# Gate and up projections of a SwiGLU FFN: 2x2 block products of seven half products, with weight sums on GpSimd

## The chip, the cores and the metric

One core of one Trainium2 chip runs the whole program. The metric is the device time of one launch in microseconds (us), lower is better. The kernel before was timed in three runs. TensorE is PE in the profile (PEld is its weight load), VectorE is DVE, ScalarE is ACT, GpSimd is POOL, SyncE is SP; an engine's name with a q is its queue of DMA issues.

## The reference, cut to what matters

A decoder layer works on 2048 prompt rows and on 32 sample rows (8 sequences of 4 tokens), with 1024 features. The part that changes is the FFN, hidden width 2816 (22 tiles of 128):

```python
gate, up = jnp.split(_rmsnorm(h, g_ffn) @ w_ffn_in, [D_FF], axis=-1)
y = h + (jax.nn.silu(gate) * up) @ w_ffn_out
```

Before it stand a norm, one input projection, sliding-window attention beside a gated linear recurrence (the mixers), and an output projection; after it a final norm.

## The kernel before

**Blocks.** Features lie on the 128 partitions and positions on the free axis. The prompt is worked in NB = 4 blocks of T = 512 positions. The 32 sample columns ride along as columns 512 to 543 in two places: in the first block's head (the `head(0, True)` of the five engines' programs: q, k and v of the samples are computed there and wait in columns T:W) and in the last block's mixers, output projection and FFN. A block of W = 544 columns is called wide, and each of its products is made in two halves of 272 columns.

**Units.** All dense products are units: 128 output features, `kt_of[u]` input tiles (8, or 7 or 8 in the down projection). A block has 90 of them: 6 in the head (k, v, four q), 8 in the mixers, 8 of the output projection (`U_O`), and the FFN in three chunks (`FCH` = 8, 7, 7 hidden tiles): for every hidden tile one gate unit and one up unit (`U_IN`), then eight down-projection units (`U_OUT`). Numbers are 32-bit: each operand is split into a high part (fp32r, made by ACT) and a low part (the rest, made by DVE), and an input tile takes three matmuls, high by high, high by low, low by high (L533 to L535 in `gemm`). A unit of eight tiles is thus 24 matmuls of 512 columns, or 48 of 272 in a wide block.

**Weights.** SP loads each unit's 512 KB into one of two buffers of `w_raw` (L404), ACT copies it to `w_hi` (L883, a ring of three), DVE subtracts it to `w_lo` (L1157). On ACT and DVE the split of unit u + 3 stands behind the work on unit u, in an order written out by hand. Semaphores count up and each engine waits for fixed counts.

**FFN.** PE runs the units without other work between (`ffn`, on PE). DVE takes the gate unit out of PSUM while it multiplies by `rinv`, the inverse root mean square (L1170), ACT takes the tanh (L1099), DVE makes tanh + 1 times gate (L1553), takes out up (L1170), multiplies (L1557), ACT and DVE split the result into `a_hi` (L1102) and `a_lo` (L1561). The down projection is added to `hT` (L1563).

**Output projection.** DVE adds bias and residual (`hT`, L1406); `h_tile` squares it on ACT (L907), adds the squares on DVE (L1180) and splits g * h into `x_hi` (L908) and `x_lo` (L1194), the FFN's input. `rinv` comes later, from a product of the summed squares with ones (`feature_sums`, L544), a root on ACT and a reciprocal on DVE (L1203).

**POOL** only sets memory and issues DMAs: `x_tok` of the next block (L420), the caches and states, the small outputs.

## Time and profile before

| What | Value |
|---|---|
| median of three runs | 2334.68 us (2333.93 to 2334.83) |
| span of the profiled execution | 2331.0 us |
| PE, DVE, ACT, POOL busy | 97%, 56%, 38%, 1% of the span |
| HBM traffic | 206 MB, 88 GB/s over the span |

The profiled execution is told by its span, from its first instruction to its last; what lies around it is not in the profile, and the median of the runs is 3.7 us above it. The page names idle time and what ended it. Records of matmuls are pipelined: a matmul's busy time is longer than the distance to the next start, so the pace of a stream is read from starts or from counts in a window.

### The profile page before, as it was taken

What the parts mean: (1) busy time and instruction counts of PE and PEld (TensorE: products, weight loads), DVE (VectorE), ACT (ScalarE), POOL (GpSimd) and SP (SyncE); (2) the same over time, 40 slices, a digit from 0 to 9 for tenths busy, and PEclk for the clock granted to TensorE, in tenths of its full rate; (3) what the DMA queues carried; (4) which work ended last, traced back from release to release, by engine and by line L of the source; (5) the groups of instructions that cost most, each with busy time, mean ns of one, the idle gap of its engine ahead of it and who ended that gap; (6) DMA issues with size and microseconds to landing.
All of it is one profiled execution on the core that took longest, in us unless ns stands there. A gap on an engine that the chain in (4) does not pass through costs nothing.

```text
span 2331.0 us, 31209 instructions
## 1 busy us (share of the span) xinstructions
PE 2251.5 (97%) x12165; PEld 1915.8 (82%) x12165; DVE 1302.4 (56%) x2146; ACT 878.1 (38%) x1349; POOL 32.4 (1%) x66
## 2 busy tenths in 40 slices
PE   6999999999999999999999999999999899999996
PEld 6777888888777888888877788888888799999996
DVE  4786535356587544445668653545668665444453
ACT  4574223235375322223457432323446532222221
POOL 1000000000000000000000000000000000000000
PEclk9999999999999999999999999999999899999998
DMA  4123232323313233332322323233231122222221
GB/s 148 55 68 114 91 100 90 101 89 92 101 46 118 91 97 93 92 98 92 107 67 63 119 91 98 91 97 94 92 124 45 30 91 86 87 91 82 92 80 60
DMA packets 58586, 207.34 MB, mean 89 GB/s; under 512 B 7341, under 2 KB 7549, under 8 KB 58416
## 3 DMA queue, kind: packets, MB, share of 16 engines
q1 hardware_dynamic: 51840, 184.57, 25.5%
q0 software_dynamic: 3936, 12.03, 1.5%
q10 hardware_dynamic: 2656, 8.62, 1.0%
q8 instruction: 104, 1.70, 0.3%
q14 instruction: 50, 0.41, 0.1%
HBM read 196.44 MB, written 9.77 MB: 88 GB/s over the span
## 4 chain that ended last, share of the span: by engine, by line
PE 84%; DVE 9%; ACT 4%; issue 2%; DMA 1%; ACTq 0%; DVEq 0%; POOL 0%
PE bank L533 27%; PE bank L535 27%; PE bank L534 27%; DVE s_p L1258 2%; DVE w_lo L1157 1%; DVE xc L1297 1%; PE bank L661 1%; ACT s_p L961 1%; DVE om L1326 1%; PE bank L628 1%; DVE pT L1277 1%; PE bank L583 1%; ACT L986 0%; PE bank L557 0%; DVE ii L1325 0%
## 5 line engine op out<-in xcount | busy, mean ns | idle before, releaser
L533 PE MATMUL bank<-x_hi,w_hi 128*128 128x512 f32 (+1 forms) x2320 | 826.4, 356 | 3.7 <-DVE x_lo L1187 2.6
L535 PE MATMUL bank<-x_hi,w_lo 128*128 128x512 f32 (+1 forms) x2320 | 820.3, 354 | 0.0
L534 PE MATMUL bank<-x_lo,w_hi 128*128 128x512 f32 (+1 forms) x2320 | 819.5, 353 | 0.0
L883 ACT ACTIVATE w_hi<-w_raw 128x1024 fp32r<-128x1024 f32 (+1 forms) x360 | 374.1, 1040 | 1175.3 <-PE bank L535 1175.3
L533 PEld LDWEIGHTS bank<-x_hi,w_hi 128*128 128x128 f32 x2320 | 438.9, 189 | 79.8 <-issue 13.6
L1157 DVE TENSOR_TENSOR w_lo<-w_raw,w_hi 128x1024 fp32r<-128x1024 f32 (+1 forms) x360 | 431.8, 1200 | 127.7 <-ACT w_hi L883 125.9
L534 PEld LDWEIGHTS bank<-x_lo,w_hi 128*128 128x128 f32 x2320 | 439.1, 189 | 61.8 <-issue 1.4
L535 PEld LDWEIGHTS bank<-x_hi,w_lo 128*128 128x128 f32 x2320 | 438.3, 189 | 60.8
L533 PE MATMUL bank<-a_hi,w_hi 128*128 128x512 f32 (+1 forms) x1200 | 427.4, 356 | 6.2 <-DVE a_lo L1561 1.8
L535 PE MATMUL bank<-a_hi,w_lo 128*128 128x512 f32 (+1 forms) x1200 | 425.0, 354 | 0.0
L534 PE MATMUL bank<-a_lo,w_hi 128*128 128x512 f32 (+1 forms) x1200 | 424.3, 354 | 0.0
L533 PEld LDWEIGHTS bank<-a_hi,w_hi 128*128 128x128 f32 x1200 | 227.6, 190 | 40.6 <-DVE a_lo L1345 3.2
L535 PEld LDWEIGHTS bank<-a_hi,w_lo 128*128 128x128 f32 x1200 | 227.3, 189 | 31.3
L534 PEld LDWEIGHTS bank<-a_lo,w_hi 128*128 128x128 f32 x1200 | 227.7, 190 | 30.5
L1563 DVE TENSOR_TENSOR hT<-bank,hT 128x512 f32<-128x512 f32 (+1 forms) x120 | 70.9, 591 | 235.5 <-PE bank L535 235.3
L1170 DVE TENSOR_TENSOR a<-bank,rinv 128x512 f32<-128x512 f32 (+1 forms) x110 | 65.1, 591 | 229.4 <-PE bank L535 227.6
L1170 DVE TENSOR_TENSOR gt<-bank,rinv 128x512 f32<-128x512 f32 (+1 forms) x110 | 65.0, 591 | 206.4 <-PE bank L535 206.0
L961 ACT ACTIVATE s_p<-s_p,nm 128x256 f32<-128x256 f32 x128 | 63.6, 498 | 51.5 <-DVE sd L1264 51.5
L661 PE MATMUL bank<-v_tok,pT 128*128 128x64 f32 x512 | 63.2, 278 | 8.3 <-ACT a_tok L998 8.3
L661 PEld LDWEIGHTS bank<-v_tok,pT 128*128 128x128 f32 x512 | 61.9, 197 | 10.8 <-issue 10.4
L1102 ACT ACTIVATE a_hi<-a 128x512 fp32r<-128x512 f32 (+1 forms) x88 | 56.3, 639 | 37.0 <-DVE a L1557 35.0
L1557 DVE SCALAR_TENSOR_TENSOR a<-gt,a 128x512 f32<-128x512 f32 (+1 forms) x88 | 61.7, 701 | 3.0
(240 smaller groups left out, 1475.0 us busy)
## 6 DMA issues: line engine op xcount, KB each, us to landing
w_raw<-in_units SPq DMA_DIRECT2D x296, 512.0 KB, 3.5
w_raw<-in_units SPq DMA_DIRECT2D x64, 448.0 KB, 3.3
x_tok<-in_x_prompt POOLq DMA_DIRECT2D x16, 512.0 KB, 6.1
out_y_p<-y_tok ACTq DMA_DIRECT2D x16, 512.0 KB, 3.0
gfin<-in_g_fin POOLq DMA_DIRECT2D x1, 512.0 KB, 7.1
kc_tok<-in_cache_k POOLq DMA_DIRECT2D x1, 512.0 KB, 6.9
vc_tok<-in_cache_v POOLq DMA_DIRECT2D x1, 512.0 KB, 7.3
out_nk_s<-in_cache_k POOLq DMA_DIRECT2D x1, 496.0 KB, 6.5
```

The lines of the kernel that those rows point to most:

```text
L533: nc.tensor.matmul(out, h, hi[:, kt, c0:c1], start=(first and kt == kts[0]), stop=False)
L534: nc.tensor.matmul(out, h, lo[:, kt, c0:c1], start=False, stop=False)
L535: mm = nc.tensor.matmul(out, l, hi[:, kt, c0:c1], start=False, stop=(kt == kt_of[u] - 1))
L661: mm = nc.tensor.matmul(V[:, head * HEAD:(head + 1) * HEAD], pT[:, s % 2, 2 * hh + half, :], v_tok[:, qb + half, g * HEAD:(g + 1) * HEAD], ...
L883: w_hi_ready.by(A(w_hi[:, u % RING, 0:n], w_raw[:, u % RAW, 0:n], ACT.Copy))
L961: A(s_p[:, s % 2, hh, :], s_p[:, s % 2, hh, :], ACT.Exp, bias=nm[:, s % 2, hh:hh + 1], accum_out=rs[:, s % 2, hh:hh + 1])
L1102: act_hi.by(A(a_hi[:, f, 0:w], a32[:, n % 2, 0:w], ACT.Copy))
L1157: w_ready.by(TT(w_lo[:, u % RING, 0:n], w_raw[:, u % RAW, 0:n], w_hi[:, u % RING, 0:n], ALU.subtract))
L1170: return lambda src, c0, c1: TT(dst(c0, c1), src, rinv[:, c0:c1], ALU.mult)
L1258: ins = nc.vector.tensor_tensor_reduce(s_p[:, s % 2, hh, :], S[g][:, jj * 256:(jj + 1) * 256], d[:, :], 2.0 ** -(head + 1), sinks[:, head: ...
L1557: act_f.by(STT(out=a32[:, n % 2, 0:w], in0=gt[:, 0:w], scalar=0.5, in1=a32[:, n % 2, 0:w], op0=ALU.mult, op1=ALU.mult))
L1563: evacuate(b, last, u, lambda src, c0, c1: TT(hT[:, m, c0:c1], src, hT[:, m, c0:c1], ALU.add))
```

## The change

Per hidden tile, gate and up weights (two tiles of 128 features, each with input tiles 0 to 3 and 4 to 7) form a 2x2 block matrix, and the normalized input (input tiles 0 to 3 and 4 to 7, first and second half of the columns) another. The four blocks of the result, gate and up of either half of the columns, are made from seven half products instead of eight, each of four input tiles, twelve matmuls and 256 columns (272 in the last block). Named by weight block: `b1` are the gate's two blocks (products p1, p2), `b22` one of up (p3), and `t1` to `t4` differences and sums of blocks (p5, p6, p7, p4). The inputs of the seven, `xo_hi` and `xo_lo` (seven operands of four tiles by half the columns), are made once in a block, in `h_tile` of the output projection, whose tiles now come in `M_ORDER`.

POOL makes the four weight sums of each hidden tile (`weight_sums`: one instruction of 128x1024, two of 128x512) and scales up by `rinv` (`scale_up`, 128x512). PE adds up p1, p6, p7 and p4 in one PSUM bank; between them ACT copies out p1, p1 + p6 and p5 (`keep`) and the full sum (`keep_c21`), and DVE adds kept values to banks (`c11`, `c12`, `c22`). The weight ring becomes six halves, and splits are made by piece: seven halves of 512 columns for each hidden tile (3584 columns of high and of low part) where two units of 1024 columns (2048) were split before.

`FCH` becomes 6, 8, 8. Two more raw buffers (`w_raw2`) lie where the mixers' temporaries are. The transposed `x_tok` of the next block is loaded by ACT's queue behind the last hidden tile, the first one's behind `ident` and `vec`, and the next block's transposes start at the third unit of the last down projection (`X_AT`). The sample columns leave the first block's head, which becomes 512 wide, for the last block's head, which becomes 544 wide: `x_s` is loaded and transposed at the end of the block before it.

```diff
+HALVES = 6
+M_ORDER = (0, 4, 1, 5, 2, 6, 3, 7)
...
+    FCH = []
+    left = NF
+    while left:
+        FCH.insert(0, min(KT, left))
+        left -= FCH[0]
...
+        SUMS = ((S[0], S[1], TB[1]), (G[0], G[1], G[2]))
...
+            def weight_sums(b, g):
+                n = load_of["g", g, 0]
+                raw_landed(pool, b, n)
+                raw_landed(pool, b, n + 1)
...
+                t13_done.by(TT(t_w[:, T1:T3 + 1:T3 - T1, 0:KH * P],
+                               both[:, 1, :].rearrange("p (o q) -> p o q", o=2), both[:, 0:2, 0:KH * P], ALU.subtract))
+                t13_done.wait(pool, b, g + 1)
+                t2_done.by(TT(t_w[:, T2, 0:KH * P], t_w[:, T1, 0:KH * P], both[:, 1, KH * P:], ALU.subtract))
+                t2_done.wait(pool, b, g + 1)
+                w_ready.wait(pool, b, max(piece_of["b1", g], piece_of.get(("t4", g - 1), 0)) + 1)
+                t4_done.by(TT(t_w[:, T4, 0:KH * P], t_w[:, T2, 0:KH * P], both[:, 0, KH * P:], ALU.add))
+            def scale_up(b, g, last):
+                w = W if last else T
+                c12_ready.wait(pool, b, g + 1)
+                u = t_w[:, up_at[g % 2], 0:w]
+                up_ready.by(TT(u, u, rinv[:, 0:w], ALU.mult))
...
+            def product(b, last, g, name, out, xo, start=False, kts=range(KH)):
+                key, half = {"p1": ("b1", 0), "p2": ("b1", 1), "p6": ("t21", 0), "p5": ("t21", 1), "p7": ("t3", 0),
+                             "p3": ("b22", 0), "p4": ("t4", 0)}[name]
+                w = H if last else T // 2
+                w_ready.wait(pe, b, piece_of[key, g] + 1)
+                at = (half_of[key, g] + half) % HALVES * KH * P
+                for kt in kts:
+                    if g == 0:
+                        xo_ready.wait(pe, b, 4 * kt + {A11: 1, S3: 2, A12: 3, A22: 3}.get(xo, 4))
+                    h = w_hi[:, at + kt * P:at + (kt + 1) * P]
+                    l = w_lo[:, at + kt * P:at + (kt + 1) * P]
+                    x_h, x_l = xo_hi[:, xo, kt, 0:w], xo_lo[:, xo, kt, 0:w]
+                    nc.tensor.matmul(out[:, 0:w], h, x_h, start=(start and kt == 0), stop=False, skip_group_check=True)
+                    nc.tensor.matmul(out[:, 0:w], h, x_l, start=False, stop=False, skip_group_check=True)
+                    mm = nc.tensor.matmul(out[:, 0:w], l, x_h, start=False, stop=(kt == KH - 1), skip_group_check=True)
+                if kts[-1] == KH - 1:
+                    prod_done.by(mm)
+            def group(b, last, ci, g):
+                a, bb, cc = SUMS[g % 2]
+                if g == 0:
+                    gates_read.wait(pe, b, LC)
+                    sc_read.wait(pe, b, NUN)
+                    pTb_ready.wait(pe, b, NUN)
+                    if last:
+                        pe.wait_ge(smp_dve, SMP_DVE_OUT)
+                elif g == 1:
+                    freed.wait(pe, b, UD0)
+                elif g == F0[ci] + 1:
+                    freed.wait(pe, b, UD0 + KT * ci)
+                if g > 1:
+                    c21_kept.wait(pe, b, g - 1)
+                product(b, last, g, "p1", a, A11, True)
+                if g > 1:
+                    c11_ready.wait(pe, b, g - 1)
+                if g == 0:
+                    early, late = range(KH - 1), [KH - 1]
+                    product(b, last, g, "p2", cc, A12, True, early)
+                    p1_kept.wait(pe, b, g + 1)
+                    product(b, last, g, "p6", a, S2, False, early)
+                    product(b, last, g, "p5", bb, S1, True, early)
+                    product(b, last, g, "p2", cc, A12, True, late)
+                    product(b, last, g, "p6", a, S2, False, late)
+                    sqh_added.wait(pe, b, KT)
+                    amix_ready.wait(pe, b, QB)
+                    stath_done.by(feature_sums(last))
+                    product(b, last, g, "p5", bb, S1, True, late)
+                else:
+                    product(b, last, g, "p2", cc, A12, True)
+                    if g > F0[ci]:
+                        finish(b, last, g - 1)
+                    p1_kept.wait(pe, b, g + 1)
+                    product(b, last, g, "p6", a, S2)
+                    if g > 1:
+                        c12_ready.wait(pe, b, g - 1)
+                    product(b, last, g, "p5", bb, S1, True)
+                u2_kept.wait(pe, b, g + 1)
+                product(b, last, g, "p7", a, S3)
+                p5_kept.wait(pe, b, g + 1)
+                product(b, last, g, "p3", bb, S4)
...
+            def finish(b, last, g):
+                c22_ready.wait(pe, b, g + 1)
+                product(b, last, g, "p4", SUMS[g % 2][0], A22)
...
+            for m in range(QB):
+                x_in.by(act.dma_start(x_tok[:, m, :], x_p[0, m * P:(m + 1) * P, :]))
...
+                        g = F0[ci] + f
+                        split(b, ("t3", g))
+                        keep(g, "p1", p1s, c11_ready, p1_kept)
+                        split(b, ("b22", g))
+                        if f > 0:
+                            keep_c21(g - 1)
+                        if f < nf - 1:
+                            split(b, ("b1", g + 1))
+                        keep(g, "p6", u2s, c12_ready, u2_kept)
+                        if g == 0:
                             stath_done.wait(act, b, 1)
                             rms(last, stdh_ready)
...
+                        split(b, ("t4", g))
+                        if f > 0:
+                            gate(g - 1)
+                        keep(g, "p5", p5s, c22_ready, p5_kept)
+                        if f < nf - 1:
+                            split(b, ("t21", g + 1))
+                        else:
+                            split(b, ("u", U_OUT[ci][0]))
+                        if f > 0:
+                            hidden_hi(g - 1, f - 1)
+                    split(b, ("u", U_OUT[ci][1]))
+                    keep_c21(g)
+                    if ci == NCH - 1 and not last:
+                        for m in range(QB):
+                            x_in.by(act.dma_start(x_tok[:, m, :], x_p[0, bass.ds((b + 1) * T + m * P, P), :]))
...
+                    gate(g)
+                    split(b, ("u", U_OUT[ci][2]))
+                    hidden_hi(g, nf - 1)
...
+                h, k = w // 2, m % KH
+                add_square(b, wide, M_ORDER.index(m), ssum, sq[:, 0], sqh_ready, sqh_added)
+                n = 4 * k
+                if m < KH:
+                    xs_ready.by(TT(x_d[:, 0:h], hT[:, m, 0:h], hT[:, m, h:w], ALU.subtract))
+                    xo_hi_ready.wait(dve, b, n + 1)
+                    xo_ready.by(STT(out=xo_lo[:, A11, k, 0:h], in0=hT[:, m, 0:h], scalar=v(VG2 + m),
+                                    in1=xo_hi[:, A11, k, 0:h], op0=ALU.mult, op1=ALU.subtract))
+                    xo_hi_ready.wait(dve, b, n + 2)
+                    xo_ready.by(STT(out=xo_lo[:, S3, k, 0:h], in0=x_d[:, 0:h], scalar=v(VG2 + m),
+                                    in1=xo_hi[:, S3, k, 0:h], op0=ALU.mult, op1=ALU.subtract))
+                    return
+                g1 = v(VG2 + k)
+                s1, s2, s4 = (x_s_[:, i, 0:h] for i in range(3))
+                ins = TS(x_g[:, 0:w], hT[:, m, 0:w], v(VG2 + m), None, ALU.mult)
+                xs_ready.by(ins)
+                xs_ready.wait(dve, b, 3 * k + 2)
+                link(STT(out=s1, in0=hT[:, k, h:w], scalar=g1, in1=x_g[:, h:w], op0=ALU.mult, op1=ALU.add))
+                link(STT(out=s2, in0=hT[:, k, 0:h], scalar=g1, in1=s1, op0=ALU.mult, op1=ALU.subtract))
+                xs_ready.by(TT(s4, x_g[:, 0:h], s2, ALU.add))
+                xo_hi_ready.wait(dve, b, n + 3)
+                xo_ready.by(TT(xo_lo[:, A12:A22 + 1, k, 0:h], x_g[:, 0:w].rearrange("p (o q) -> p o q", o=2),
+                               xo_hi[:, A12:A22 + 1, k, 0:h], ALU.subtract))
+                xs_ready.wait(dve, b, 3 * k + 3)
+                xo_hi_ready.wait(dve, b, n + 4)
+                xo_ready.by(TT(xo_lo[:, S1:S4 + 1, k, 0:h], x_s_[:, :, 0:h], xo_hi[:, S1:S4 + 1, k, 0:h],
+                               ALU.subtract))
...
+                def add(g, name, n, dst, kept_as, kept, ready):
+                    prod_done.wait(dve, b, prod_of[name, g])
+                    kept.wait(dve, b, g + 1)
+                    ready.by(TT(dst, SUMS[g % 2][n][:, 0:h], kept_as, ALU.add))
+                def c11(g):
+                    if g == 0:
+                        xo_ready.wait(dve, b, 4 * KH)
+                    add(g, "p2", 2, gt[:, g % 2, 0:h], p1s, p1_kept, c11_ready)
+                def c22(g):
+                    add(g, "p7", 0, t_w[:, up_at[g % 2], h:w], p5s, p5_kept, c22_ready)
+                def c12(g):
+                    add(g, "p3", 1, t_w[:, up_at[g % 2], 0:h], u2s, u2_kept, c12_ready)
+                def gate(g):
+                    c21_kept.wait(dve, b, g + 1)
+                    c11_ready.wait(dve, b, g + 1)
+                    gate_ready.by(TT(gt[:, g % 2, 0:w], gt[:, g % 2, 0:w], rinv[:, 0:w], ALU.mult))
+                def hidden(g):
+                    gate_tanh.wait(dve, b, g + 1)
+                    link(STT(out=gt[:, g % 2, 0:w], in0=th[:, 0:w], scalar=1.0, in1=gt[:, g % 2, 0:w],
+                             op0=ALU.add, op1=ALU.mult))
+                    up_ready.wait(dve, b, g + 1)
+                    act_f.by(STT(out=a32[:, g % 2, 0:w], in0=gt[:, g % 2, 0:w], scalar=0.5,
+                                 in1=t_w[:, up_at[g % 2], 0:w], op0=ALU.mult, op1=ALU.mult))
+                def hidden_lo(g, f):
+                    act_hi.wait(dve, b, g + 1)
+                    act_ready.by(TT(a_lo[:, f, 0:w], a32[:, g % 2, 0:w], a_hi[:, f, 0:w], ALU.subtract))
                 for ci, nf in enumerate(FCH):
...
+                    for f in range(nf):
+                        g = F0[ci] + f
+                        split(b, ("t3", g))
+                        split(b, ("b22", g))
+                        c11(g)
+                        if f > 0:
+                            gate(g - 1)
+                        if f < nf - 1:
+                            split(b, ("b1", g + 1))
+                        if g == 0:
                             invert(b, last, stdh_ready)
...
+                        split(b, ("t4", g))
+                        if f > 0:
+                            hidden(g - 1)
+                        c22(g)
+                        if f < nf - 1:
+                            split(b, ("t21", g + 1))
+                        else:
+                            split(b, ("u", U_OUT[ci][0]))
+                        if f > 0:
+                            hidden_lo(g - 1, f - 1)
+                        c12(g)
...
+            mixers(NB - 2, False)
+            ffn(NB - 2, False, True)
+            head(NB - 1, True, NB - 2)
```

## Rows read from the trace of the kernel before

**Rows 1.** Page, busy time, share of the span and instructions of each engine.

```profile
PE 2251.5 (97%) x12165; PEld 1915.8 (82%) x12165; DVE 1302.4 (56%) x2146; ACT 878.1 (38%) x1349; POOL 32.4 (1%) x66
```

**Rows 2.** Page, the chain that ended last, share of the span by engine.

```profile
PE 84%; DVE 9%; ACT 4%; issue 2%; DMA 1%; ACTq 0%; DVEq 0%; POOL 0%
```

**Rows 3.** Windows: length, busy per engine (count), granted clock, DMA share, GB/s.

```profile
225.00:345.00 120.00, 120.00 (x518) 97.01 (x517) 54.36 (x66) 31.40 (x36) 0.00 (x0) 1.00 0.31 97
...
2110.00:2290.00 180.00, 178.69 (x1419) 178.25 (x1418) 84.39 (x127) 45.30 (x55) 0.00 (x0) 1.00 0.27 83
```

**Rows 4.** Lines by form, PE: busy, mean ns | idle before, releaser.

```profile
L533 PE MATMUL bank<-x_hi,w_hi 128*128 128x512 f32 x1392 | 555.0, 399 | 0.0
...
L533 PE MATMUL bank<-x_hi,w_hi 128*128 128x272 f32 x928 | 271.4, 292 | 3.7 <-DVE x_lo L1187 2.6 <-DVE x_lo L1194 1.2
...
L644 PE MATMUL bank<-ident,s_p 128*128 128x128 f32 x256 | 35.2, 282 | 7.8 <-ACT es L963 6.3 <-DVE pnT L1468 1.0 <-DVE kc_T L1433 0.4
```

**Rows 5.** Timeline of PE: start, length; 24 starts apart, 21 starts apart, eight transposes.

```profile
91.62 1.04 PE L644 MATMUL bank<-ident,s_p 128*128 128x128 f32 x8
...
250.05 0.39 PE L533 MATMUL bank<-x_hi,w_hi 128*128 128x512 f32 x1
...
255.62 0.39 PE L533 MATMUL bank<-x_hi,w_hi 128*128 128x512 f32 x1
...
2000.08 0.29 PE L533 MATMUL bank<-x_hi,w_hi 128*128 128x272 f32 x1
...
2002.73 0.29 PE L533 MATMUL bank<-a_hi,w_hi 128*128 128x272 f32 x1
```

**Rows 6.** Timeline of DVE in the last block, one tile pair apart.

```profile
2110.47 0.44 DVE L1170 TENSOR_TENSOR a<-bank,rinv 128x272 f32<-128x272 f32 x1 [2.50 <-PE bank L535]
...
2122.55 0.44 DVE L1170 TENSOR_TENSOR a<-bank,rinv 128x272 f32<-128x272 f32 x1 [2.50 <-PE bank L535]
```

**Rows 7.** Lines by form, DVE and ACT, in the FFN.

```profile
L1157 DVE TENSOR_TENSOR w_lo<-w_raw,w_hi 128x1024 fp32r<-128x1024 f32 x296 | 362.1, 1223 | 109.8 <-ACT w_hi L883 108.0
...
L883 ACT ACTIVATE w_hi<-w_raw 128x1024 fp32r<-128x1024 f32 x296 | 313.1, 1058 | 950.7 <-PE bank L535 950.7
...
L1561 DVE TENSOR_TENSOR a_lo<-a,a_hi 128x512 fp32r<-128x512 f32 x66 | 45.1, 684 | 0.0
...
L1561 DVE TENSOR_TENSOR a_lo<-a,a_hi 128x544 fp32r<-128x544 f32 x22 | 15.8, 718 | 0.0
...
L1563 DVE TENSOR_TENSOR hT<-bank,hT 128x272 f32<-128x272 f32 x48 | 21.2, 441 | 66.9 <-PE bank L535 66.8
...
L1102 ACT ACTIVATE a_hi<-a 128x512 fp32r<-128x512 f32 x66 | 41.8, 633 | 34.1 <-DVE a L1557 34.1
...
L968 ACT ACTIVATE pT<-bank 128x512 f32<-128x512 f32 x32 | 18.6, 580 | 0.3 <-PE bank L644 0.3
...
L1099 ACT ACTIVATE th<-gt 128x512 f32<-128x512 f32 x66 | 40.7, 617 | 10.2 <-DVE gt L1170 10.2
```

**Rows 8.** Waits: who waited for whom, total us, times, longest.

```profile
ACT w_hi L883 <- PE bank L535: 1175.3, 316, 6.5
```

**Rows 9.** Lines of POOL: its largest elementwise instruction.

```profile
L423 POOL MEMSET gates_w<- 128x1024 f32 x1 | 1.0, 977 | 0.0
```

**Rows 10.** Lines by form, the tail of the output projection.

```profile
L1406 DVE SCALAR_TENSOR_TENSOR hT<-bank,vec,xT 128x512 f32<-128x512 f32 x24 | 18.0, 750 | 29.5 <-PE bank L535 29.5
...
L907 ACT ACTIVATE sq<-hT 128x512 f32<-128x512 f32 x24 | 14.9, 619 | 3.5 <-DVE hT L1406 3.4
```

**Rows 11.** Chain of the start: start, length, what.

```profile
5.12 8.61 DMA xs_tok<-in_x_sample
...
13.87 1.03 PE bank L831 x8
```

**Rows 12.** DMA issues: count, KB each, us from issue to landing.

```profile
x_tok<-in_x_prompt POOLq DMA_DIRECT2D x16, 512.0 KB, 6.1
...
vec<-in_vecs ACTq DMA_DIRECT2D x1, 37.0 KB, 8.0
```

More of the change, by code:

```diff
@@ L559, in x_T, with xs_T @@
                 xT_done.by(mm)
+            def xs_T(b):
+                pe.wait_ge(xs_in, 16 * DT)
+                stdh_ready.wait(pe, b, 1)
+                for kt in range(KT):
+                    mm = nc.tensor.transpose(V[:, kt * NS:(kt + 1) * NS], xs_tok[:, kt * P:(kt + 1) * P],
+                                             ident[0:NS, 0:NS])
+                smp_by(mm)
             def values_T(n):
@@ L734, in mixers @@
                 rest = ahead
-                for u in U_O[rest:]:
-                    gemm(b, last, u, a_hi, a_lo)
+                for i in range(rest, KT):
+                    gemm(b, last, UO0 + i, a_hi, a_lo)
             def sample_load(b, s):
@@ L932, in head @@
                 if wide:
-                    split(n, U_K + RING)
+                    ahead(n, U_K)
                 freed.wait(act, n, U_K + 1)
@@ L1130, in _ @@
                 chain.restart()
+            mixers(NB - 2, False)
+            ffn(NB - 2, False, True)
+            head(NB - 1, True, NB - 2)
             b = NB - 1
@@ L1611, in _ @@
                 chain.restart()
+            mixers(NB - 2, False)
+            ffn(NB - 2, False, True)
+            head(NB - 1, True, NB - 2)
             b = NB - 1
```

635 lines of the change are left out of this document (420 added, 215 removed).

## The prediction

> **What bounds the kernel now.** I read the page's busy shares first, then its chain, then windows and waits. PE is busy for 97% of the span, DVE for 56%, ACT for 38%, POOL for 1% [rows 1], and PE carries 84% of the chain that ended last [rows 2]. In the FFN the windows show a PE without idle time at a granted clock of 1.00, that is the 2.4 GHz level, with DVE at 45% and ACT at 26% [rows 3]. ACT spent 1175.3 us waiting, before its weight copies, for matmuls to let go of a buffer [rows 8]: the weight path runs ahead and waits for PE. So a stage of the FFN lasts as long as its matmuls do, as long as the other engines stay inside PE's time.
>
> **PE, what goes and what comes.** The 512-column stream has 518 matmuls in 120.00 us, 0.2317 us each [rows 3]; two starts 24 matmuls apart give 5.57 us, 0.2321 each [rows 5]. A hidden tile (gate and up unit) is 48 of them, 11.12 us. In the last block a tile pair takes 2122.55 - 2110.47 = 12.08 us [rows 6] for 96 matmuls of 272 columns, 0.1258 us each; two starts 21 apart say 0.1262 [rows 5]. The change makes 7 products of 4 input tiles and 3 matmuls, 84 in all.
>
> In the last block they are 272 wide, the form of the rows: 84 x 0.1258 = 10.57 us, 1.51 less per tile, x 22 = 33 us.
>
> In the other blocks they are 256 wide, and no row has that form. The straight line through the two forms has a slope of (0.2317 - 0.1258) / 240 columns and gives 0.1187 us. Bounds: half of the 512 form, 0.1159, and the 272 form itself, 0.1258. I take 0.1187, since 256 lies 16 columns from the 272 row. A matmul now has its own weight load for half as many columns; that this doesn't bind is seen in the mixers, where eight transposes of 128 columns, each with a load, end 1.04 us after the first start, hence start at most 0.15 apart, and with the last one's own 0.28 us [rows 4] taken off 0.11 [rows 5]. So 84 x 0.1187 = 9.97 us, 1.15 less, x 66 tiles of three blocks = 76 us. At the bounds: 36 us and 92 us. PE's gain in sum is 109 us, between 69 and 125.
>
> **Weight path and ACT per tile.** Before, two splits of 1024 columns; after, two of 1024 and three of 512. ACT: 2 x 1.06, 3 x 0.63 (a 512-column copy), four copies of 256 PSUM columns at 0.58 at most (the 512 form), tanh 0.62, high part 0.63 [rows 7]: 2.12 + 1.89 + 2.32 + 1.25 = 7.6 us of 9.97. DVE: splits 2 x 1.22 + 3 x 0.68 = 4.5; gate, two hidden steps and the low part, 4 x 0.68 = 2.7; three additions from PSUM at 0.44 (the 272 form) = 1.3 [rows 7]: 8.5 us of 9.97, where it was 5.9 of 11.12 (two splits, five of 0.68). Nothing is left to spare on DVE but 1.5 us, so the cover that costs these at nothing is thin: what overruns 9.97 us is paid in full.
>
> **PE's new waits.** Order on PE: p1, p2, p4 of the tile before, p6, p5, p7, p3, each twelve matmuls or 1.42 us. p6 waits for ACT's copy of p1: p2 and p4 lie between, 2.85 us for a wait of 0.6 (split t3 is ahead of it on ACT and ready early). p7 waits for the copy of p1 + p6, with p5 between, 1.42 us; behind the full sum of the tile before stand split b1 (1.06) and then this copy, which fits. p3 waits for the copy of p5, with p7 between; ahead of it on ACT stand split t4 and the tanh, 0.63 + 0.62 after the copy at 0.4: the tanh needs DVE's gate step, which itself waits for ACT's copy of the full sum. It fits by about half a us. p4 waits for DVE's c22 with a whole p3, p1 and p2 between, 4.3 us. I cost all this at 0.05 us per tile, 4 us; bounds 0, and 0.5 us per tile, 44 us (what the tightest hand-off is short of slack for).
>
> **First tile of a block.** Its inputs come from the last tile of the output projection. After PE's end there: hT 0.75, square 0.62 [rows 10], sum 0.68, x_g 0.68, three of 256 columns at 0.44 = 1.3; then ACT copies 768 columns (between 0.63 and 1.06, say 0.85), splits t3 (0.63) and only then copies p1 (0.4) [rows 7]: 5.9 us. PE has p1 and three quarters of p2, 1.42 + 1.07 = 2.5 us, and stands at the wait for p1. That is 3.4 us, four times 14 us, where the wait on x_lo was 1.2 us once [rows 4]: +13 us, bounds 8 and 20. The low parts of the inputs, 0.68 and 0.95 more on DVE, run beside ACT.
>
> **Chunk ends.** After the last p4: copy 0.4, gate 0.68, tanh 0.62, two hidden steps 1.4, high 0.63, low 0.68, together 4.4 us. PE has the first five or seven input tiles of two units, 30 or 42 matmuls, 7.0 or 9.7 us. Nothing, if DVE is in time.
>
> **Queues and edges.** SP brings 1 MB per tile in 9.97 us as against 11.12: the DMA share was 0.31 [rows 3], nothing. ACT issues the four `x_tok` loads: they stood on POOL, landed in 6.1 us [rows 12], and have two units, 11 us, before the first transpose. On ACT they delay the gate's tanh by four issues: inside the chunk end's slack. At the start PE no longer waits for `xs_tok`, which landed at 13.7 [rows 11], but `vec` is still issued and took 8.0 us, and `x_tok` now stands behind it on ACT's queue [rows 12]: I take 0, bounds -5 and +5. The head that loses 32 columns and the head that gains them cancel; eight small transposes of 1.03 us [rows 11] move.
>
> **POOL.** Per tile 128x1024, and three times 128x512: 2560 columns, two inputs each. The trace has only memsets, 0.98 us for 1024 columns [rows 9]. Bounds: as a memset, 2.5 us; three times that (two reads, one write), 7.4 us. I take twice, 4.9 us; all lie inside 9.97 us, and its waits (DVE's splits of t3 and t4) come once per tile with slack. The sums have a tile's lead.
>
> **Sum.** 2331.0 - 109 + 13 + 4 = 2239 us of span; the median of the runs stands 3.7 above the span: 2243 us.
>
> **Rivals.**
>
> *DVE and POOL hinder each other (slower).* DVE has 7.2 us per tile of instructions with two inputs in SBUF, POOL 4.9 us that read SBUF. If one holds the other off for as long as it runs, a tile can't be shorter than 7.2 + 4.9 = 12.1 us: 0.98 x 66 = 65 us more, in the last block, with DVE's four 544-column steps at 0.72 [rows 7], 12.3 against 12.08, 5 us more, and the 13: 2331 + 83 + 4 = 2418 us. It decides from a POOL share of 4.0 us per tile on (7.2 + 4.0 = 11.2, where the gain of 69 to 125 us is gone); with the lower bound of POOL's price (9.7) it costs nothing, with the upper one (14.6) some 300 us. For it: DVE is the engine nearest to full, and nothing in this profile has POOL reading SBUF. Against: no row shows an instruction of one engine stretched by another's.
>
> The Trainium skill, SBUF — State Buffer, on contention between engines, says that a DVE instruction with two SBUF inputs and a GpSimd instruction that reads SBUF exclude each other for the whole instruction. By that rule this rival is what happens; no row here can show it. The Trainium skill's GPSIMD Engine Reference, section 3.1, gives 4497 ns for a two-input instruction of 2048 columns, by which POOL's part would be 5.6 us and this rival's time about 2475 us, an estimate.
>
> *The gain is half eaten (faster, but less).* Either the 256-column matmul costs as much as the 272 one (-69 us, 2282 us), or the copies between products come late by up to 0.5 us per tile (2283 us), or DVE and POOL hinder each other only in part (a tile of 10.5 to 11: 2280 to 2325 us). For it: DVE at 85% with waits on three engines.
>
> **How the numbers follow.** Forecast case (PE bound, own range 2222 to 2270): 0.48. Half eaten: 0.18. No change: 0.03. Slower: 0.31, a port shared for whole instructions. I don't give the last more, since its size hangs on a POOL price that rows leave between 2.5 and 7.4 us. A difference within 0.2% (4.7 us) can't be told from none. Faster is 0.48 + 0.18 = 0.66, same 0.03, slower 0.31. The range from 2224 to 2430 leaves out the lower edge of the forecast case (0.04) and of the slower case what lies above 2430 (about 0.14).
>
> **What would show it.** Right: 84 starts of the 256-column form about 0.119 us apart; a tile pair every 10.0 us; PE without idle time between tiles, but some 3 us of it at each block's first tile, released by ACT's copy of p1; DVE's 1024-column split still at 1.22 us. Wrong by the port: that split or POOL's sums stretched while the other runs, PE waiting on w_lo or on a copy, the granted clock perhaps falling behind such waits. Wrong by hand-offs: PE idle before p7 or p3, released by ACT, with durations unchanged.

## The result, and the profile after

The changed kernel takes 2405.39 us (median of 4 runs, 2404.31 to 2409.24) beside 2334.30 us for the kernel before (4 runs, 2333.40 to 2334.83): ratio 1.031, 95% interval 1.0295 to 1.0324. It is 3.1% slower. The forecast of 2243 us and its direction were wrong. The time lies inside the stated range only because that range also took in the slower rival (2418 us). The profiled execution has a span of 2403.4 us, 2.0 below the median.

The page after, its busy shares and its chain; they answer to [rows 1] and [rows 2]:

```profile
PE 2200.8 (92%) x14277; PEld 1986.5 (83%) x14277; DVE 1901.3 (79%) x2678; ACT 1155.8 (48%) x2021; POOL 700.6 (29%) x402
...
PE 47%; DVE 33%; issue 13%; ACT 5%; DMA 1%; ACTq 0%; DVEq 0%; POOL 0%
```

PE has less to do than before but isn't full any more. DVE's busy time grew by 599 us, and its part of the chain from 9% to 33%. The same two windows as in [rows 3] (length, busy time of PE, PEld, DVE, ACT and POOL, granted clock, DMA share, GB/s):

```profile
225.00:345.00 120.00, 112.43 (x780) 104.23 (x780) 101.28 (x109) 54.08 (x93) 55.14 (x30) 0.99 0.32 93
2110.00:2290.00 180.00, 167.49 (x1274) 165.28 (x1272) 146.09 (x154) 75.06 (x128) 83.71 (x43) 0.97 0.29 87
```

The first window holds 780 matmuls in 120 us, where the forecast pace of 0.1187 us would give 1011. The pace itself is as forecast. On PE's timeline (start, length) 40 matmuls of 256 columns separate the first two starts, 4.73 us or 0.1183 us each. Then PE stands until ACT has copied p5:

```profile
241.41 0.28 PE L1053 MATMUL bank<-xo_lo,w_hi 128*128 128x256 f32 x1
...
246.14 0.28 PE L1054 MATMUL bank<-xo_hi,w_lo 128*128 128x256 f32 x1
248.60 0.38 PE L1052 MATMUL bank<-xo_hi,w_hi 128*128 128x256 f32 x1 [2.17 <-ACT t_w L1437]
```

PE's waits after (total us, times, longest):

```profile
PE bank L1052 <- ACT t_w L1437: 105.0, 65, 4.5
PE bank L782 <- DMA x_tok<-in_x_prompt: 17.2, 1, 17.2
PE bank L1052 <- DVE xo_lo L1618: 10.9, 3, 3.7
...
PE bank L1052 <- DVE xo_lo L1637: 8.1, 2, 4.5
```

The largest one names ACT, but ACT isn't late by itself: its copy of p5 stands behind the tanh, which waits for DVE's gate step. So I read DVE's timeline of one whole hidden tile (start, length):

```profile
267.65 0.68 DVE L1557 TENSOR_TENSOR w_lo<-t_w,w_hi 128x512 fp32r<-128x512 f32 x1
268.25 1.78 DVE L1557 TENSOR_TENSOR w_lo<-w_raw,w_hi 128x512 fp32r<-128x512 f32 x1
269.95 0.41 DVE L1990 TENSOR_TENSOR gt<-bank,t_w 128x256 f32<-128x256 f32 x1
270.29 2.56 DVE L2006 TENSOR_TENSOR gt<-gt,rinv 128x512 f32<-128x512 f32 x1
272.77 2.28 DVE L1557 TENSOR_TENSOR w_lo<-w_raw,w_hi 128x1024 fp32r<-128x1024 f32 x1
...
276.30 1.67 DVE L2013 SCALAR_TENSOR_TENSOR a<-gt,t_w 128x512 f32<-128x512 f32 x1
...
280.29 0.68 DVE L1557 TENSOR_TENSOR w_lo<-t_w,w_hi 128x512 fp32r<-128x512 f32 x1
```

And POOL's in the same stretch:

```profile
267.81 1.68 POOL L647 TENSOR_TENSOR t_w<-t_w,rinv 128x512 f32<-128x512 f32 x1 [3.03 <-DVE t_w L1990]
269.44 2.86 POOL L634 TENSOR_TENSOR t_w<-w_raw 128x1024 f32<-128x1024 f32 x1
272.38 1.59 POOL L637 TENSOR_TENSOR t_w<-t_w,w_raw 128x512 f32<-128x512 f32 x1
275.74 1.67 POOL L640 TENSOR_TENSOR t_w<-t_w,w_raw 128x512 f32<-128x512 f32 x1 [1.77 <-DVE w_lo L1557]
280.45 1.68 POOL L647 TENSOR_TENSOR t_w<-t_w,rinv 128x512 f32<-128x512 f32 x1 [3.04 <-DVE t_w L1990]
```

From 267.65 to 280.29 DVE has no idle time: a tile is 12.64 us, and DVE fills it. Four of its instructions are long, and each has a POOL instruction that started before it; DVE's ends 0.54 us after POOL's end for 512 columns (269.49 and 270.03) and 1.08 us after it for 1024 (273.97 and 275.05), a little less than its undisturbed 0.68 and 1.22. The one of 1.78 us has the size of the one of 0.68 us ahead of it. Against undisturbed rows of the same size the four are 1.10, 1.88, 1.06 and 0.98 us too long, in sum 5.0 us; without that the tile would be 7.6 us on DVE. POOL is held too: 1.67 us for sums that take 1.28 at the shortest. The split of 1024 columns, L1157 of [rows 7] at 1223 ns, and the 512-column forms, by form over the kernel (busy, mean ns):

```profile
L1557 DVE TENSOR_TENSOR w_lo<-w_raw,w_hi 128x512 fp32r<-128x512 f32 x112 | 181.1, 1625 | 11.1 <-ACT w_hi L1197 11.1
L1557 DVE TENSOR_TENSOR w_lo<-w_raw,w_hi 128x1024 fp32r<-128x1024 f32 x76 | 154.5, 2032 | 6.5 <-ACT w_hi L1197 6.5
L2006 DVE TENSOR_TENSOR gt<-gt,rinv 128x512 f32<-128x512 f32 x66 | 140.4, 2127 | 3.4 <-ACT gt L1442 3.2
L1557 DVE TENSOR_TENSOR w_lo<-t_w,w_hi 128x512 fp32r<-128x512 f32 x200 | 139.0, 700 | 1.4 <-ACT w_hi L1197 1.0
...
L1990 DVE TENSOR_TENSOR t_w<-bank,t_w 128x256 f32<-128x256 f32 x132 | 54.5, 413 | 0.0
```

The additions that take one input from PSUM (last row) stay at 0.41 us. In the last block the same instructions are stretched, and two scale ups stand 2123.72 - 2110.79 = 12.93 us apart, where a pair took 12.08 [rows 6].

### The profile page after: what moved, and what is told of

The parts are those of the page before. It is cut to its first block, busy times and chain, and to the rows that moved or that the text cites. A ratio compares the mean times of both kernels' runs of the same rounds, so it can differ in the third digit from the quotient of the medians.

```text
span 2403.4 us, 38939 instructions
## 1 busy us (share of the span) xinstructions
PE 2200.8 (92%) x14277; PEld 1986.5 (83%) x14277; DVE 1901.3 (79%) x2678; ACT 1155.8 (48%) x2021; POOL 700.6 (29%) x402
## 4 chain that ended last, share of the span: by engine, by line
PE 47%; DVE 33%; issue 13%; ACT 5%; DMA 1%; ACTq 0%; DVEq 0%; POOL 0%
PE bank L758 10%; PE bank L760 10%; PE bank L759 10%; DVE w_lo L1557 9%; DVE gt L2006 7%; PE bank L1052 5%; PE bank L1054 4%; PE bank L1053 4%; DVE s_p L1701 2%; DVE w_lo L1553 1%; DVE a_lo L2018 1%; DVE gt L2010 1%; DVE t_w L1990 1%; DVE gt L1990 1%; PE bank L895 1%
## 5 line engine op out<-in xcount | busy, mean ns | idle before, releaser
L1052 PE MATMUL bank<-xo_hi,w_hi 128*128 128x256 f32 (+1 forms) x2464 | 728.5, 296 | 124.8 <-ACT t_w L1437 105.0
L1053 PE MATMUL bank<-xo_lo,w_hi 128*128 128x256 f32 (+1 forms) x2464 | 715.4, 290 | 0.0
L1054 PE MATMUL bank<-xo_hi,w_lo 128*128 128x256 f32 (+1 forms) x2464 | 715.0, 290 | 0.0
L1052 PEld LDWEIGHTS bank<-xo_hi,w_hi 128*128 128x128 f32 x2464 | 482.8, 196 | 147.9 <-ACT t_w L1437 61.2
L634 POOL TENSOR_TENSOR t_w<-w_raw 128x1024 f32<-128x1024 f32 x88 | 244.3, 2776 | 890.9 <-DMA w_raw<-in_units 725.7
L1054 PEld LDWEIGHTS bank<-xo_hi,w_lo 128*128 128x128 f32 x2464 | 484.0, 196 | 0.0
L1053 PEld LDWEIGHTS bank<-xo_lo,w_hi 128*128 128x128 f32 x2464 | 482.5, 196 | 1.1 <-issue 0.7
L1557 DVE TENSOR_TENSOR w_lo<-w_raw,w_hi 128x512 fp32r<-128x512 f32 (+1 forms) x188 | 335.6, 1790 | 17.7 <-ACT w_hi L1197 17.6
L1557 DVE TENSOR_TENSOR w_lo<-t_w,w_hi 128x512 fp32r<-128x512 f32 (+1 forms) x276 | 232.4, 845 | 10.8 <-ACT w_hi L1197 10.4
L758 PE MATMUL bank<-x_hi,w_hi 128*128 128x512 f32 (+1 forms) x560 | 205.1, 366 | 1.5 <-DVE x_lo L1604 1.5
```

Of the source, the lines that this page charges most:

```text
L634: t13_done.by(TT(t_w[:, T1:T3 + 1:T3 - T1, 0:KH * P], both[:, 1, :].rearrange("p (o q) -> p o q", o=2), both[:, 0:2, 0:KH * P], ALU.subtract))
L758: nc.tensor.matmul(out, h, hi[:, kt, c0:c1], start=(first and kt == kts[0]), stop=False)
L1052: nc.tensor.matmul(out[:, 0:w], h, x_h, start=(start and kt == 0), stop=False, skip_group_check=True)
L1053: nc.tensor.matmul(out[:, 0:w], h, x_l, start=False, stop=False, skip_group_check=True)
L1054: mm = nc.tensor.matmul(out[:, 0:w], l, x_h, start=False, stop=(kt == KH - 1), skip_group_check=True)
L1557: ins = TT(w_lo[:, lo:hi].rearrange("p (o q) -> p o q", o=k), src[:, o:o + k, :], w_hi[:, lo:hi].rearrange("p (o q) -> p o q", o=k), ALU.s ...
```

## The experiments

Theory A is the rival: a DVE instruction with two inputs in SBUF and a POOL instruction that reads SBUF hold each other off for whole instructions. Against it stood that POOL's sums come too late for ACT and PE, whatever they read (theory B), and the order of ACT's work, the tanh ahead of the copy of p5 (theory C). The reference for the first four runs is 2332.86 us for the kernel before (7 runs).

**1. POOL keeps its place and its busy time, but hardly reads.** Each 512 columns of a sum, and each scale up, become one column of addition and 24 to 32 small memsets to the same tile. This leaves out the weight sums and the up scaling.

```diff
-                t2_done.by(TT(t_w[:, T2, 0:KH * P], t_w[:, T1, 0:KH * P], both[:, 1, KH * P:], ALU.subtract))
+                writes(t_w[:, T2, :], KH * P, 24, t2_done)
```

> The changed kernel with POOL's four two-input instructions per hidden tile replaced by small memsets of the same outputs, some 1.3 us for each 512 columns, so that POOL stays about as busy but reads only one column (the weight sums and the scaling of up are left out: the values are constants). Theory A, DVE and POOL hold each other off at the read side: DVE's 512-column split and its gate step go back from 1.6 to 2.5 us to 0.68, the tile pair from 12.65 to about 10.0, the whole to 2250 to 2280 us. Theory B, POOL's sums come too late for ACT and PE whatever they read: the tile stays within 0.5 us of 12.65 and the time within 40 us of 2405. Theory C, the hand-off order alone (PE waits for the copy of p5, which stands behind the tanh): no gain, 2395 to 2410.

Measured: 2243.71 us (2 runs), ratio 0.9617 (0.9598 to 0.9636), 6 us under the expected range. The page's busy shares, and the rows of DVE and POOL by form:

```profile
PE 2145.2 (96%) x14277; PEld 1949.5 (87%) x14277; DVE 1541.8 (69%) x2678; ACT 1151.1 (51%) x2021; POOL 767.9 (34%) x11754
```

```profile
L1561 DVE TENSOR_TENSOR w_lo<-w_raw,w_hi 128x1024 fp32r<-128x1024 f32 x152 | 185.5, 1221 | 53.3 <-ACT w_hi L1201 52.0
...
L1565 DVE TENSOR_TENSOR w_lo<-w_raw,w_hi 128x512 fp32r<-128x512 f32 x112 | 76.0, 687 | 14.5 <-ACT w_hi L1205 13.6
...
L624 POOL MEMSET t_w<- 128x21 f32 x5984 | 433.6, 113 | 0.0
```

POOL is busy for 67 us more than after the change, and DVE's 512-column split falls from 1625 to 687 ns, so theory B falls. Is it because POOL only writes, or because its instructions are short? Rows of DVE and POOL from the same stretch (their timelines):

```profile
239.98 0.69 DVE L2018 SCALAR_TENSOR_TENSOR gt<-th,gt 128x512 f32<-128x512 f32 x1
```

```profile
239.44 1.28 POOL L624 MEMSET t_w<- 128x21 f32 x24
240.81 0.63 POOL L622 TENSOR_TENSOR t_w<-ones 128x1 f32<-128x1 f32 x1
```

The 24 memsets take 1.28 us with DVE's two-input instruction in their middle, as they do where DVE is mostly idle (at 242.94), and DVE keeps its 0.69. The one-column addition, which reads, takes 0.63 beside DVE's next two-input instruction and 0.19 where DVE is idle (at 242.82). And such a row of memsets isn't too short to hold DVE: one instruction with a single tile as input, `x_g`, it does hold (last section). So for DVE's two-input instructions it is reading that counts. A tile, from one tanh on ACT to the next, is 9.94 us in this block:

```profile
239.09 0.62 ACT L1455 ACTIVATE th<-gt 128x512 f32<-128x512 f32 x1
249.03 0.62 ACT L1455 ACTIVATE th<-gt 128x512 f32<-128x512 f32 x1
```

In the first chunk of the second and third block some take 10.3 to 10.8 us; there ACT waits for the last memsets (4.3 us once), which belongs to this run alone, since run 9 has 9.94 there. The loss against the forecast is gone with POOL's reads: 2243.71 us beside 2243. That the two agree to the microsecond is partly luck, as the next section shows.

**2. ACT copies p5 ahead of the tanh.**

```diff
                         split(b, ("t4", g))
+                        keep(g, "p5", p5s, c22_ready, p5_kept)
                         if f > 0:
                             gate(g - 1)
-                        keep(g, "p5", p5s, c22_ready, p5_kept)
```

> The changed kernel with one line moved: ACT copies p5 before it makes the tanh of the tile before. Theory C, the order on ACT costs the 2.5 us that PE stands there: the tile goes to about 10.3 us and the time to about 2240. Theory A, DVE has no idle time left in a tile (12.65 us of its own and waiting for the port), so the 2.5 us turn up at another wait of PE: 2390 to 2406.

Measured: 2403.16 us (2 runs), ratio 1.0301 (1.028 to 1.0321), the same as the changed kernel. The wait only changes its name, from ACT's copy to DVE's split:

```profile
PE bank L1052 <- DVE w_lo L1557: 90.5, 56, 2.2
```

Theory C falls. The releaser of PE's largest wait was a messenger.

**3. Sums and scaling on DVE, POOL idle.** The same four instructions per tile, spread over DVE's own order, with the same result.

```diff
+                        sum13(b, g + 1)
                         split(b, ("b1", g + 1))
...
+                    link(TT(u, u, rinv[:, 0:w], ALU.mult))
```

> The changed kernel with the three weight sums and the scaling of up moved from POOL to DVE; POOL has no elementwise work in the FFN. Theory A: DVE's tile loses 5 us of waiting and gains 1.14 + 3 x 0.60 = 2.9 us of work, 7.7 + 2.9 = 10.6 us, so about 2 us less than now for some 19 intervals of each block: 2250 to 2275 us, faster than both kernels. Theory B or C: DVE was full at 8.5 us before and gets 3 us more, so the tile is at least 12.65: 2405 or slower.

Measured: 2292.48 us (2289.43 to 2296.43), ratio 0.9828 (0.9812 to 0.9845): 1.7% under the kernel before and 113 us under the changed one, although DVE does more. It misses the expectation by 17 to 42 us. DVE's timeline:

```profile
242.27 0.69 DVE L2006 TENSOR_TENSOR t_w<-t_w,rinv 128x512 f32<-128x512 f32 x1
...
252.94 0.69 DVE L2006 TENSOR_TENSOR t_w<-t_w,rinv 128x512 f32<-128x512 f32 x1
```

A tile is 10.67 us, without idle time on DVE in between: DVE's own sum, 0.73 above PE's 9.94. The same scaling cost 1.68 us of POOL and 1.10 of DVE before, and 0.69 here. So the tile came as expected (10.6); what was off is the number of tiles. The expectation took 19 of a block at the full 2 us, but only 13 (3, 5 and 5 in the three chunks) were 12.6 us and more after the change; in the others a chunk begins or ends, and at the end POOL has no next sums to make. The start was also 6.3 us later than in the changed kernel (the first block's reciprocal at 47.97 instead of 41.69 us); run 8 takes that up.

**4. Only the scaling on DVE.**

```diff
-                            scale_up(b, g - 1, last)
...
+                    link(TT(u, u, rinv[:, 0:w], ALU.mult))
```

> Only the scaling of up (one 512-column instruction per tile) moves from POOL to DVE. Theory A: DVE loses the 1.1 us that its b22 split waits behind it and gains 0.6: tile about 12.1, time about 2365 us. Theory B or C: DVE gets more work and nothing back, 2405 to 2440.

Measured: 2370.03 us (2 runs), ratio 1.0159 (1.0138 to 1.0179), 5 us from the expected 2365. The tile is 254.12 - 241.88 = 12.24 us from one sum of POOL to the next:

```profile
241.88 2.78 POOL L634 TENSOR_TENSOR t_w<-w_raw 128x1024 f32<-128x1024 f32 x1 [4.35 <-DVE w_lo L1554]
...
254.12 2.79 POOL L634 TENSOR_TENSOR t_w<-w_raw 128x1024 f32<-128x1024 f32 x1 [4.36 <-DVE w_lo L1554]
```

**5. Only the sums on DVE.** The other half of run 3.

```diff
-                            weight_sums(b, g + 1)
...
+                            sum13(b, g + 1)
...
+                            sum2(b, g + 1)
...
+                            sum4(b, g + 1)
```

> The four weight sums move to DVE, the up scaling stays on GpSimd (1.7 us a tile beside DVE). Port exclusion: a hidden tile costs DVE 2.4 us of sums in place of some 5.6 to 6 us of holding, and keeps 1.7 us of holding by the scaling; with the version that has everything on DVE at 10.67 us a tile, this one stands at 10.67 - 0.69 + about 1.3 to 1.7 = 11.3 to 11.7 us, so 2292 + 75 x 0.65 to 1.0 = 2340 to 2370 us. If instead only the amount of GpSimd work counted and the two ran side by side, a tile would be 9.98 us and the time near 2245 to 2255 us. Scaling alone moved gave 2370 us, so the two moves should together explain 2405 to 2292.

Measured: 2315.59 us, ratio 0.9921 (0.9904 to 0.9937), 24 us under the expected range. The kernel before of runs 5 to 8 took 2332.76 us (9 runs). DVE's and POOL's timelines:

```profile
247.03 0.68 DVE L1530 TENSOR_TENSOR w_lo<-t_w,w_hi 128x512 fp32r<-128x512 f32 x1
247.63 1.81 DVE L1530 TENSOR_TENSOR w_lo<-w_raw,w_hi 128x512 fp32r<-128x512 f32 x1
```

```profile
247.20 1.70 POOL L624 TENSOR_TENSOR t_w<-t_w,rinv 128x512 f32<-128x512 f32 x1 [9.37 <-DVE t_w L1993]
258.26 1.68 POOL L624 TENSOR_TENSOR t_w<-t_w,rinv 128x512 f32<-128x512 f32 x1 [9.37 <-DVE t_w L1993]
```

The tile is 258.26 - 247.20 = 11.06 us: less than the 11.3 to 11.7 that I expected, since one POOL instruction stretches one DVE instruction by 1.1 us and no more. Against the changed kernel the scaling alone is worth 35 us (run 4) and the sums alone 90 us; both together gave 113 us (run 3). In a full tile they add up: 12.64 - 12.24 = 0.40 and 12.64 - 11.06 = 1.58 us, together the 1.97 of run 3. The 12 us between the sum of the two runs and run 3 lie mostly in the first interval between two tanhs of the second and third chunk: 12.7 us after the change, 11.2 in run 4, and already 9.97 in run 5 and 9.94 in run 3, where PE's own time is the bound and nothing more can be had.

**6. Run 3 with ACT's copy of p5 ahead of the tanh**, the edit of run 2 in the kernel of run 3.

```diff
+                        keep(g, "p5", p5s, c22_ready, p5_kept)
                         if f > 0:
                             gate(g - 1)
```

> Everything on DVE, and ACT copies p5 ahead of the tanh. With everything on DVE a hidden tile is 10.67 us because DVE's own instructions fill it (242.27 to 252.94 us, no idle time in it), not because of a wait of TensorE on ACT. Bound by DVE's sum: no change, 2290 to 2295 us. If the tanh held TensorE's bank: 0.4 us a tile, 2260 to 2270 us.

Measured: 2295.34 us (2292.68 to 2298.95), ratio 0.9842 (0.9825 to 0.9858). No change. With POOL idle too, the order of ACT's work decides nothing.

**7. The other direction: POOL reads in the kernel before.** POOL adds two tiles of SBUF into tiles that nobody reads then, five times for each of 45 hidden tiles.

```diff
+                        for i in range(5):
+                            scr.wait(pool, b, n)
+                            out = (ra, ii, qq, om)[i % 4]
+                            scr.by(nc.gpsimd.tensor_tensor(out[:, :], gl[:, 0, :], gl[:, 1, :], ALU.add))
```

> The kernel before, with five additions 128x512 of two SBUF tiles on GpSimd in each of the 15 hidden tiles of the first two chunks of the first three blocks, written to tiles that nobody reads then: 45 tiles with some 6.4 us of GpSimd each. Port exclusion: DVE's split 128x1024 (1223 ns) and 128x512 (684 ns) show means of 1.5 us and more and 1.0 us and more in those stretches, the additions take over 1.4 us each, and DVE's 5.9 us and GpSimd's 6.4 us of a tile no longer fit in TensorE's 11.1 us: up to 1.2 us a tile, 2334 + 0 to 55 us = 2335 to 2390 us, likeliest 2360. Without exclusion: DVE's means unchanged and 2333 us.

Measured: 2341.62 us (2337.91 to 2342.59, 6 runs), ratio 1.0036 (1.0023 to 1.0048). From 225 to 500 us DVE's lines by form, and from one timeline DVE's split and POOL beside it:

```profile
L1169 DVE TENSOR_TENSOR w_lo<-w_raw,w_hi 128x1024 fp32r<-128x1024 f32 x43 | 78.0, 1814 | 9.8 <-ACT w_hi L895 9.8
L1565 DVE SCALAR_TENSOR_TENSOR gt<-th,gt 128x512 f32<-128x512 f32 x17 | 26.9, 1582 | 0.0
...
L1182 DVE TENSOR_TENSOR a<-bank,rinv 128x512 f32<-128x512 f32 x17 | 11.8, 692 | 18.0 <-PE bank L547 17.9
```

```profile
271.26 2.14 DVE L1169 TENSOR_TENSOR w_lo<-w_raw,w_hi 128x1024 fp32r<-128x1024 f32 x1 [0.40 <-ACT w_hi L895]
```

```profile
271.02 1.30 POOL L457 TENSOR_TENSOR ra<-gl 128x512 f32<-128x512 f32 x1 [2.85 <-DVE gt L1182]
272.40 2.15 POOL L457 TENSOR_TENSOR ii<-gl 128x512 f32<-128x512 f32 x1
```

The same stretching appears in a kernel that the change hasn't touched: the split means 1814 ns instead of 1223, while an instruction with one input in PSUM keeps its 692. Over the kernel DVE is busy for 180 us more, 4.0 us for each of the 45 tiles. Yet it costs 9 us in all, not the 25 that I held likeliest; 5.9 us of PE's waits, 1.8 before, are for the low part `a_lo` in front of a down projection. The tile stays at 11.15 us (two gate steps at 270.17 and 281.32), since DVE had 5 us to spare in it. So the stretching is no price by itself; it becomes one where DVE's own time plus what it is held reaches PE's.

**8. Run 3, with POOL's constants and cache copies issued behind the prompt tokens.** At the start the changed kernel waits 17.2 us for `x_tok`, run 3 23.8.

```diff
+            x_in.wait(pool, 0, QB)
             for dst, src in ((dist[:, :], dist_in[0]), (dist_b[:, :], dist_in[1]), (sinks[:, :], sinks_p),
```

> Everything on DVE, and GpSimd issues its constants and cache copies only when the prompt tokens have landed. If the first transposes are late because some 2 MB of other transfers share the DMA engines with the 2 MB of tokens, the first matmul stands 3 to 5 us earlier and the time is 2287 to 2290 us. If the tokens' own issue is what is late, nothing changes, or the constants land late for the mixers.

Measured: 2285.22 us (2279.55 to 2288.01), ratio 0.9791 (0.9772 to 0.981), 7 us under run 3 and 2 under the expected range. PE's wait:

```profile
PE bank L745 <- DMA x_tok<-in_x_prompt: 14.1, 1, 14.1
```

The first reciprocal stands at 38.39 us, 9.6 earlier than in run 3, where 3 to 5 were expected; 3 us of that are lost again over the later blocks, and why wasn't tried. So POOL's transfers, issued at the same time, are what made the tokens late in run 3; the same edit in the changed kernel wasn't tried. Why run 3 was 6.3 us later at this point than the changed kernel, with the same issues on ACT's and POOL's queues, stays open; in its trace SP's first weight load is issued at 3.37 us instead of 1.07.

**9. Run 8, with the up scaling taken out of the hidden tile.** Scaling columns and the down projection can change places: the down product is scaled by `rinv` when it is added to `hT`, in a stage where DVE idles.

```diff
-                    link(TT(u, u, rinv[:, 0:w], ALU.mult))
...
+                def out_add(m, u, src, c0, c1):
+                    if c0 == 0:
+                        freed.wait(dve, b, u)
+                    o = th[:, c0:c1]
+                    link(TT(o, src, rinv[:, c0:c1], ALU.mult))
+                    return TT(hT[:, m, c0:c1], o, hT[:, m, c0:c1], ALU.add)
```

> The version with everything on DVE and the start order, in which the up half isn't scaled in the hidden tile: the down product is scaled when it is added to hT, 24 more DVE instructions of 0.69 us a block in the down stages, 22 fewer in the hidden tiles. Port exclusion plus DVE's sum as the bound: a tile falls from 10.67 us to about 9.98, TensorE's own 9.97, and the down stages, where DVE idles, don't grow: 2285.2 - 75 x 0.65 = about 2236 to 2245 us. If a hidden tile was held by a chain between the engines and not by DVE's sum, the time stays within 5 us of 2285.

Measured: 2246.71 us (2243.19 to 2248.51, 5 runs) beside 2332.50 us (9 runs), ratio 0.9631 (0.9618 to 0.9644): the best version with the full computation, 3.7% under the kernel before. The time is 1.7 us above the expected range. The tanh comes every 9.94 us, PE's own pace as in run 1, and PE is full again:

```profile
PE 2144.8 (96%) x14277; PEld 1948.0 (87%) x14277; DVE 1793.1 (80%) x3062; ACT 1158.3 (52%) x2021; POOL 24.2 (1%) x50
```

```profile
237.07 0.62 ACT L1410 ACTIVATE th<-gt 128x512 f32<-128x512 f32 x1
247.01 0.62 ACT L1410 ACTIVATE th<-gt 128x512 f32<-128x512 f32 x1
```

DVE is busy for 80% of the span here and for 79% in the changed kernel: the same share, once useful and once partly waiting.

**10. Run 9 with ACT's copy of p5 ahead of the tanh**, the edit of run 2 once more.

```diff
+                        keep(g, "p5", p5s, c22_ready, p5_kept)
                         if f > 0:
                             gate(g - 1)
-                        keep(g, "p5", p5s, c22_ready, p5_kept)
```

> The same with ACT's copy of p5 ahead of the tanh. With DVE no longer the bound, the copy of p5 may be what TensorE waits for next: 0.1 to 0.3 us a tile, so 5 to 20 us under the kernel with the other order, where that wait is seen; equal to it within 3 us where DVE still fills the tile.

Measured: 2247.67 us (2245.23 to 2252.49), ratio 0.9633 (0.962 to 0.9646). No change a third time, although DVE no longer fills the tile: the tanh comes every 9.94 us with either order, so PE had no wait for the copy of p5 that could be saved.

## Why the prediction was wrong

**The step that failed** is the one on POOL: 4.9 us a tile, "all lie inside 9.97 us". That is true of POOL's own timeline and false of its effect. The section costed POOL by whether it would be in time and never charged DVE for it, while the section on DVE had found only 1.5 us to spare there and said that what overruns is paid in full. The two sections had to be added: DVE's 7.6 us and the 5.0 it is held make 12.6. DVE's own 8.5 us of the forecast were 0.9 too many, since it added up whole rows and each instruction starts some 0.08 us before the row ahead of it ends; without that slip the cover would have been 2.4 us instead of 1.5, and still too thin for 5.0.

**The price of POOL** was too low as well: 1.28 us for 512 columns and 2.39 for 1024 are the shortest rows, so 3 x 1.28 + 2.39 = 6.2 us undisturbed against 4.9, inside the bounds of 2.5 to 7.4. The Trainium skill, GPSIMD Engine Reference, section 3.1, comes nearer: 5.6 us is the estimate by its figure for 2048 columns, and the runs show some 11% more.

**The rival** had the mechanism, the side and nearly the size. It gave 12.1 us for a tile and 2418 us; measured are 12.64 us and 2405 us. The tile is longer, since its 7.2 us for DVE left out the additions from PSUM, which stand in line too, while part of POOL's 6.2 lies beside them. The estimate of 2475 us, with POOL at 5.6 us, should be about 2480 by the rival's own sum. The time is shorter, since not each of the 22 tiles of a block is a full one. In the third chunk the distances of the tanh are 12.67, 12.69, 12.61, 12.60, 12.69, then 10.76 and 7.36 us, where POOL has no next sums to make, and in run 1 five of 9.94, then 10.08 and 6.86. By stretches, from one reciprocal on DVE to the next, the changed kernel stands over run 1 by 150 us in the four FFNs (38.6, 38.1, 34.8, 38.7) and by 11 us in the heads, mixers and output projections: 161 in all, the difference of their spans.

**The chance was misplaced, not only the sum.** The argument against the rival was that no row shows one engine's instruction stretched by another's. But no row of the kernel before had POOL reading SBUF, so the trace could not have shown it: an absence that says nothing. The rule in the Trainium skill, SBUF — State Buffer, in its section on SBUF's two separate sides, spoke directly of this pair. The runs agree with it on each point that they touch: two-input DVE instructions and POOL's reads exclude each other (1.78 us for 0.68), while additions with one input in PSUM keep their 0.41 us beside POOL's reads and two-input splits their 687 ns beside its writes. The 0.31 was also set down because the size hung on POOL's price; but the sign didn't, from 4.0 us a tile on, and two of three figures for that price were above it.

**PE's part was right.** 0.1183 us a matmul against 0.1187, 9.94 us a tile against 9.97, and in the last block 10.59 against 10.57. The span with POOL's reads gone (run 1) is 2242.6 us against 2239; that it comes so near is partly luck. From reciprocal to reciprocal, run 1 is 108 us under the kernel before in the four FFNs, where the sum has 92 with the first tiles, and 19 over it elsewhere, where it has 0: 5.7 at the start, 13.9 between the last two blocks' FFNs, where the sample columns now pass the head, against 3.3 won in the first head, which the forecast took to cancel. These borders can shift a few us between stretches.

**First tile of a block**: the path was seen in part, and the size was too small. Over the four blocks PE waits 26.8 us there after the change and 22.0 in run 1, against 14 forecast for the wait (13 after the old one is taken off, upper bound 20). The wait before p6 is longer than its 3.4 us in three blocks (4.6 to 4.8 in run 1), and the copy of p1 and DVE's last low part land within 0.3 us of each other, so that the profile names now one, now the other. In three blocks another wait stands before it, 3.6 us (1.4 to 1.6 in run 1), for the low parts of p1's last input tile; the forecast had DVE's low parts "run beside ACT".

**New hand-offs**: 4 us forecast. In run 1 PE waits 11.3 us for ACT's copies, of which 8.0 stand at the first tiles; the other 3.3 fit. Runs 2, 6 and 10 show that the order of the copies is worth nothing.

**The start**: 0 forecast with ±5, measured 41.69 - 36.76 = 4.9 us at the first reciprocal, the upper bound. That the 2 MB of tokens share the DMA engines with POOL's loads is a cause that run 8 shows for run 3's kernel, and only makes likely here. **Chunk ends** were costed at nothing; PE waited there for `a_lo` three times, 6.2 us in sum, 5.7 in run 3, whose DVE has more to do, and 1.7 in run 1: next to nothing where DVE is as free as the forecast had it. **The granted clock** was 0.99 and 0.97 in the two windows instead of 1.00. In the last block run 1 has 0.98 without the waits and run 4 has 1.00 with them, so it isn't laid on the waits.

## What to carry to other kernels

Before work goes to an idle engine, ask what it shares with the engine that is nearest to full, and add the two engines' times where they exclude each other: here 6 us of POOL's additions cost DVE 5 us, and the same additions on DVE itself cost 3. If the trace has no row in which the two run together, it is no evidence that they can; a small run that adds such reads to the kernel as it is (run 7) answers it for little, if one reads the durations of the instructions and not the time, which moved by 9 us only. And where an engine's sum per tile is just above the bound, look for algebra that moves an instruction to a stage in which that engine idles (run 9, 38.5 us) before handing it to another engine.
